# Memory keys and the middle chunks of residual projections: high and low inputs in one 512-column matmul

## The reference, cut to what matters

```python
# first block, twice: mixer A (selected attention), then mixer B (stick breaking)
x = layer_norm(ALPHA * x + (o * silu(g)) @ w_out, ln_g, ln_b)
# second block, two layers (fourier+neighbourhood mixer, then gated convolution)
m = rms_norm_2(mem, mem_norm_g)
h = h + mixer(rms_norm_2(h, mix_g)) @ w_out
k, v = split(m @ wkv)                    # memory keys and values
h = h + softmax(q @ k.T / 16) @ v @ wo   # q from rms_norm_2(h, xa_g) @ wq
h = h + conv_ffn(rms_norm_2(h, ffn_g))
return rms_norm_2(h, final_g)
```

## Time and profile before

| | us |
|---|---|
| median of three runs | 991.11 (990.96 to 991.43) |
| span of the profiled execution | 989.2 |
| PE busy | 972.1 (98%) |
| PE weight loads busy | 879.3 (89%) |
| DVE busy | 686.6 (69%) |
| ACT busy | 556.1 (56%) |
| POOL busy | 209.3 (21%) |

### The profile page before, as it was taken

How to read it: one execution, slowest core, us unless ns; L and a number is a source line. 1 busy time by engine, 2 the same in 40 slices (tenths; PEclk the granted TensorE clock), 3 DMA queues, 4 the chain that set the end, 5 groups by cost and what they waited for, 6 DMA issues and landing times.

```text
span 989.2 us, 16695 instructions
## 1 busy us (share of the span) xinstructions
PE 972.1 (98%) x6532; PEld 879.3 (89%) x6532; DVE 686.6 (69%) x1056; ACT 556.1 (56%) x856; POOL 209.3 (21%) x199
## 2 busy tenths in 40 slices
PE   9999989999999999999999999999999999999997
PEld 8779759989988988798899899999898989989985
DVE  5789785854666687665556779776687665767973
ACT  5556673665765474555355466555445555546662
POOL 0002034300344440012003005221044301202610
PEclk9999999999999999999999999999999999999999
DMA  9634425465334447246414655457546432555441
GB/s 363 241 132 166 175 87 208 162 221 214 128 128 141 174 133 271 108 171 213 150 64 170 213 186 187 181 194 281 186 170 255 163 135 93 198 183 181 172 152 43
DMA packets 24831, 172.93 MB, mean 175 GB/s; under 512 B 2752, under 2 KB 2880, under 8 KB 4416
## 3 DMA queue, kind: packets, MB, share of 16 engines
q1 hardware_dynamic: 23040, 160.66, 45.6%
q10 hardware_dynamic: 1728, 11.40, 3.0%
HBM read 166.81 MB, written 5.24 MB: 174 GB/s over the span
## 4 chain that ended last, share of the span: by engine, by line
PE 93%; DVE 2%; ACT 2%; DMA 1%; issue 1%; POOL 0%; SPq 0%; ACTq 0%; DVEq 0%
PE banks L506 38%; PE banks L594 16%; PE banks L512 14%; PE banks L514 7%; PE banks L504 6%; PE banks L656 4%; PE banks L710 1%; DMA raw<-w 1%; PE banks L761 1%; PE banks L762 1%; DVE work L1725 1%; PE banks L743 1%; PE banks L917 1%; PE banks L834 0%; DVE work L1737 0%
## 5 line engine op out<-in xcount | busy, mean ns | idle before, releaser
L1598 DVE TENSOR_TENSOR wl<-raw,wh 128x1024 fp32r<-128x1024 f32 x300 | 379.7, 1275 | 157.4 <-ACT wh L1090 156.0
L1090 ACT ACTIVATE wh<-raw 128x1024 fp32r<-128x1024 f32 x300 | 313.2, 1054 | 180.6 <-PE banks L506 76.1
L512 PE MATMUL banks<-xx,wh 128*128 128x512 f32 x544 | 192.5, 398 | 0.0
L506 PE MATMUL banks<-xx,wh 128*128 128x256 f32 x1024 | 190.3, 284 | 0.0
L506 PE MATMUL banks<-yy,wh 128*128 128x256 f32 x1024 | 187.8, 285 | 0.1
L506 PEld LDWEIGHTS banks<-xx,wh 128*128 128x128 f32 x1024 | 161.4, 192 | 1.4 <-issue 0.5
L506 PEld LDWEIGHTS banks<-yy,wh 128*128 128x128 f32 x1024 | 160.4, 192 | 0.7 <-issue 0.5
L514 PE MATMUL banks<-xx,wl 128*128 128x256 f32 x544 | 151.8, 279 | 0.0
L506 PE MATMUL banks<-xx,wl 128*128 128x256 f32 x512 | 144.8, 283 | 0.0
L506 PE MATMUL banks<-yy,wl 128*128 128x256 f32 x512 | 138.6, 283 | 0.0
L512 PEld LDWEIGHTS banks<-xx,wh 128*128 128x128 f32 x544 | 102.0, 187 | 22.7
(11 more groups left out here) (221 smaller groups left out, 1449.3 us busy)
## 6 DMA issues: line engine op xcount, KB each, us to landing
raw<-w SPq DMA_DIRECT2D x149, 1024.0 KB, 4.8
m_scratch<-yy ACTq DMA_DIRECT2D x2, 1024.0 KB, 5.9
k_scratch<-kt ACTq DMA_DIRECT2D x2, 1024.0 KB, 8.2
kt<-k_scratch ACTq DMA_DIRECT2D x2, 1024.0 KB, 5.8
yy<-m_scratch ACTq DMA_DIRECT2D x2, 1024.0 KB, 6.0
raw<-w SPq DMA_DIRECT2D x2, 512.0 KB, 5.2
h<-xt SPq DMA_DIRECT2D x2, 512.0 KB, 6.1
v<-memt ACTq DMA_DIRECT2D x1, 1024.0 KB, 7.7
```

The source lines that it names most:

```text
L506: return pe.matmul(b[:, j, :], weights, o_[:, kk, :], start=k0 + k == 0 and q == 0 and (j == 0 or not both_open), stop=k0 + k == KT * p.de ...
L512: pe.matmul(b[:, j, :], wh[:, slot, j, k * P:k * P + P], operand[:, :, tile0 + k0 + k, :], start=k0 + k == 0, stop=False, skip_group_check ...
L1090: act.activation(wh[:, n % 2, j, :], raw[:, n % RAW_SLOTS, j, :], ACT.Copy).then_inc(hi_ready, 1)
L1598: dve.tensor_tensor(wl[:, n % 2, j, :], raw[:, n % RAW_SLOTS, j, :], wh[:, n % 2, j, :].bitcast(F32), ALU.subtract).then_inc(lo_ready, 1)
```

## The change

The stages `kx0` and `kx1` become apart. With that, the pairs of `kx0`'s and `kx1`'s neighbours move, ACT gets a copy of the low part at the end of each key chunk's list, and DVE adds before it scales. In the residual projections `oa`, `ob`, `oab`, `oc`, `ox0`, `ox1` the chunks 1 and 2 (of 0 to 3) use 512-column matmuls into banks 6, 7 and 4, 5. DVE adds both parts to `h` straight from PSUM, in two instructions in place of one. Chunks 0 and 3 stay as they were. These stages are unrolled instead of looped, and chunk 2 is no longer in the early order.

```diff
-    add("kx0", 4, "dve")
+    add("kx0", 4, "dve", apart=True)
     add("gb", 4, "dve", apart=True)
...
-    add("kx1", 4, "dve")
+    add("kx1", 4, "dve", apart=True)
...
+        MIDDLE = {1: 6, 2: 4}
+
+        def middle_banks(c):
+            q = MIDDLE[c]
+            return banks[:, q:q + 2, 0:S], banks[:, q:q + 2, S:2 * S]
...
-            def project(name, operand, ready=None, hooks={}, tile0=0):
+            def project(name, operand, ready=None, hooks={}, tile0=0, middle=False):
...
+                        joined = middle and per * i + c in MIDDLE
+                        if joined:
+                            b = banks[:, MIDDLE[per * i + c]:, :]
...
-                                if apart and not early:
+                                if (apart or joined) and not early:
                                     mm = apart_product(k, j)
...
+                elif middle:
+                    round_(0, True)
+                    round_(1, False, {}, None)
...
-            project("oa", yy, y_ready("A", g_lo, GBASE["A"], 1))
+            project("oa", yy, y_ready("A", g_lo, GBASE["A"], 1), middle=True)
...
@@ ACT, layer_norm, at the end of each c
+                    act.wait_ge(w_used, 2 * n + 2)
+                    act.activation(kt[:, 2 * c:2 * c + 2, :], apart(p, c)[1], ACT.Copy).then_inc(low_out, 1)
...
@@ DVE, residual
                         elif alpha is None:
+                            if c in MIDDLE:
+                                b, low = middle_banks(c)
+                                chain(dve.tensor_tensor(hc, low, hc, ALU.add))
                             dve.tensor_tensor(hc, b, hc, ALU.add).then_inc(dve_evac, 1)
+                        elif c in MIDDLE:
+                            b, low = middle_banks(c)
+                            chain(dve.scalar_tensor_tensor(hc, hc, alpha, b, ALU.mult, ALU.add))
+                            dve.tensor_tensor(hc, low, hc, ALU.add).then_inc(dve_evac, 1)
...
@@ DVE, layer_norm, at the end of each c
-                    dve.wait_ge(w_used, 2 * n + 2)
-                    dve.tensor_tensor(kt[:, 2 * c:2 * c + 2, :], b3(p.pair + c % 2),
-                                      rb_m[:, :].unsqueeze(1).broadcast_to([P, 2, S]), ALU.mult).then_inc(dve_evac, 1)
+                    kc = kt[:, 2 * c:2 * c + 2, :]
+                    dve.wait_ge(low_out, LBASE[filler] + c + 1)
+                    chain(dve.tensor_tensor(kc, apart(p, c)[0], kc, ALU.add))
+                    dve.tensor_tensor(kc, kc, rb_m[:, :].unsqueeze(1).broadcast_to([P, 2, S]), ALU.mult).then_inc(dve_evac, 1)
```

More of the change, by code:

```diff
@@ L187 @@
 GEBASE = bases(("ffn0", 8), ("ffn1", 8))
-LBASE = bases(("gb", 4), ("qn", 2), ("kn", 2), ("qx0", 4), ("fu0", 8), ("cb", 4), ("cc", 4), ("qx1", 4), ("fu1", 8))
+LBASE = bases(("kx0", 4), ("gb", 4), ("kx1", 4), ("qn", 2), ("kn", 2), ("qx0", 4), ("fu0", 8), ("cb", 4), ("cc", 4), ("qx1", 4), ("fu1", 8))
 ACC = bases(*[(u, 4) for u in ("mem", "mean0", "var0", "mean1", "var1", "mix0", "xa0", "ffn0", "mix1", "xa1", "ffn1")])
@@ L993, in _ @@
                     z_values(t - 6)
-            project("ob", yy, y_ready("B", g_lo, GBASE["B"], 1))
+            project("ob", yy, y_ready("B", g_lo, GBASE["B"], 1), middle=True)
             project("kx1", yy, tile0=KT, hooks=layer_norm_hooks("1"))
@@ L1036, in _ @@
                            lambda a, b: [(bank[b][:, 0:S], slice(P * a, P * a + P))], 1, pn, "vn")
-            project("oab", yy, mixer_ready)
+            project("oab", yy, mixer_ready, middle=True)
             for l in "01":
@@ L1048, in _ @@
                 if l == "1":
-                    project("oc", yy, y_ready("conv", g_lo, GBASE["conv"], 2))
+                    project("oc", yy, y_ready("conv", g_lo, GBASE["conv"], 2), middle=True)
                 def first_scores(a, l=l):
@@ L1063, in _ @@
                                1, pa, "vx" + l)
-                project("ox" + l, yy, y_ready("X" + l, dve_evac, pa.base, 2))
+                project("ox" + l, yy, y_ready("X" + l, dve_evac, pa.base, 2), middle=True)
                 project("fu" + l, xx, x_ready("ffn" + l), hooks=norm_hooks("ffn" + l))
```

## The result

| | before | after |
|---|---|---|
| median (us) | 991.11 | 1006.21 (1005.45 to 1007.29, five executions) |
| ratio of the medians | | 1.0154 (1.0143 to 1.0165) |
| span of the profiled execution (us) | 989.2 | 1005.5 |
| its own time (us) | 991.1 (span plus 1.9) | 1007.29 |

The kernel became 1.5% slower, 15.1 us by the medians. The profiled execution is the longest of its five. All five have spans of 1003.6 to 1005.5 us, at mean granted clocks of 0.994 to 0.992, and the longer ones have the lower clock. The two profiles differ by 16.3 us.

What follows compares the result with a forecast made beforehand. PE, busy 98% of the span, was taken to bound the kernel. Terms 3.4 + 6.3 + 3.8 + 2.1 - 0.2 = 15.4 us on a 989.2 us span gave 1004.6, plus 1.9 for the median: 1006.5 us, range 1000.5 to 1009.5.

Steps and rivals of the forecast that it cites:

- `gb`: entry, with `oa` and `kx0`: At `gb`, PE waits for DVE's third key evacuation and starts near 197.1 us: +3.4 us, savings in `oa` and `kx0` included.
- clock behind it: Behind the waits at `gb` and `zf`, clock falls to 1.2 GHz for 3.9 us, losing 1.9 us each, +3.8 together.
- `zf`: entry, with `ob` and `kx1`: At `zf`, PE waits for `kx1`'s third evacuation until about 367.2 us; `zf` ends at 379.2, not 372.90: +6.3 us.
- the three statistics, with their savings: After `ox0`, `oc` and `ox1`, POOL's later sum delays PE's statistic, losing 0.7 us in each place, savings included: +2.1 us.
- I take 0.1 us later for DVE's list: In `kx0`, the shift expected of DVE's instruction list before its third key evacuation: 0.1 us.
- near 371: Sign to look for: PE idle before `zf`, 7 us long, near 371 us in the new trace's own time.
- The wait for the first chunk's banks: In `kx0`, PE waits 0.5 us at about 180.7 us for the first key chunk's evacuation before the third key chunk.
- The ring: In `ox0`, `oc`, `ox1`, DVE's and ACT's lists depend on each other in a cycle; third chunk's 0.7 us delay persists.
- The ring absorbs the third chunk's delay: Rival for `ox0`, `oc`, `ox1`: that delay is hidden too, 2.7 us less, 1003.8 us; 0.30 shared with a kinder clock.
- 0.9 us of waiting for POOL: Sign to look for: the statistic in `fu0`, `qx1` and `fu1` waits 0.9 us for POOL.
- DVE falls behind in `kx`: Rival in `kx0` and `kx1`: a late `lo` stops PE, two waits of 1.6 us, 1009.7 us; chance 0.10.
- The other side: Rival at `gb` and `zf`: DVE evacuates early enough, so entries and clock cost nothing, 991.0 or 988.3 us; chance 0.08.

Runs made afterwards that it cites:

- the half fill: Changed kernel plus 14 idle-work PE matmuls of 128 columns ahead of `gb`'s wait and 30 ahead of `zf`'s; 1003.58 us, ratio 1.0127.
- Own banks: Changed kernel, but `gb`'s first chunk and `zf` sum into free banks 6 and 7, so neither entry waits for the keys; 994.55 us, ratio 1.0034.
- the keys alone: Changed kernel with the residual projections as before, so only the memory keys in `kx0` and `kx1` are apart; 1006.69 us, ratio 1.0155.
- the middle chunks alone: Kernel before with only the second and third chunk of the six residual projections joined, keys as before; 991.95 us, ratio 1.0009.
- the earlier evacuation: Changed kernel with the third key chunk's copy and evacuation moved ahead of the last lo and last two low parts; 997.66 us, ratio 1.0067.

## Why the prediction was right

The forecast was 1006.5 us and the time is 1006.21. That the two agree within 0.3 us is luck: term by term the forecast is 0.9 us short of the profiled execution, and the median lies 1.1 us below that execution. The mechanism isn't luck, since every wait that it counted is there. By its own terms, with the places of the table above (in the time of the profile, which ended 1.1 us above the median of its kernel):

| term | forecast | shown |
|---|---|---|
| `gb`: entry, with `oa` and `kx0` | +3.4 | +3.9 |
| clock behind it | +1.9 | +1.5 |
| `zf`: entry, with `ob` and `kx1` | +6.3 | +6.9 |
| clock behind it | +1.9 | +2.7 |
| the three statistics, with their savings | +2.1 | +1.7 |
| `oab` | -0.2 | -0.2 |
| start of the trace | | -0.2 |
| sum | 15.4 | 16.3 |

These are one profiled execution's. The clock's share is the difference between the changed kernel's chunks and those of the half fill (7.51 less 6.01, 8.41 less 5.75); the entries are the rest of each pair of stages (5.20 + 0.59 - 0.34 = 5.45, and 9.36 + 0.36 - 0.19 = 9.53).

- **The mechanism at both entries** was as forecast: `gb`'s first matmul at 197.26 where about 197 stood, behind the third scaling, with idle times of 3.46 and 7.33 us released by DVE. Own banks took it away and the clock's loss with it; an earlier place in DVE's list shrank both.
- **"I take 0.1 us later for DVE's list"** was too little. It is 0.4 us in this trace's time and 0.6 with the 0.2 by which the trace started earlier. The statistic was forecast to be read at 184.7 to 185.1 and is at 185.13. This is most of what the two entries have too much. In the sum for `zf`, 10.9 us for its 48 matmuls doesn't follow from the two rows: with 3.00 for 12 and 5.55 for 24, the other 12 bring it to some 11.3, and the half fill's chain has 5.75 + 5.59 for them. And the sign "near 371" leaves out the clock behind `gb`: by the forecast's own terms it was to be about 372.5, and it is 372.88.
- **The wait for the first chunk's banks** in `kx` was forecast at 0.5 us. Between the two matmuls lie 0.90 us instead of 0.12, and the next one is another 0.1 late, so 0.9. It eats all that the joined tiles of `kx` save. By the distances of PE's matmuls two smaller things come on top: in `kx0` 22 of the 53 tiles that were forecast at 347 ns go at 353, behind this wait and behind the last spread (0.15 us), and the statistics take 0.2 to 0.3 us more of PE's time between joined tiles than between tiles of three. The entry hid all this in the changed kernel, and the versions without the entry wait pay it.
- **The clock**: forecast equal in both places, from the start of the trace. It isn't: 1.5 and 2.7 us here, and 0.8 and 0.2 more in the execution with the keys alone (8.35 and 8.62 us for the same matmuls, 5.3 us of work at the low clock at `gb`). At the longer standstill it had fallen well before PE began again and was low for 5.7 us of work, at the shorter one for 3.4. A single duration taken from the start of the program was the wrong measure; the sum was right within 0.5 because one term was too high and one too low, which is luck too.
- **The ring**: forecast 0.7 net in each of three places, shown 0.62, 0.48 and 0.62 in the changed kernel. That the second chunk's delay dies out and the third's arrives was shown by joining the second alone. *The ring absorbs the third chunk's delay* is refuted. The sign "0.9 us of waiting for POOL" came out as 0.47: of the 0.83 us by which `fu0` is longer, most of the rest is lost before, in one pause of 0.26 in its first chunk.
- **The pace** of the middle chunks: 353 ns, as forecast. By the Trainium skill, page TensorE: Matmul & The Clock Gate, section "Wait — 56ns, not 53.3ns?", a warm matmul of 512 columns is followed after about 216 ns, and by its formula one of 256 after 109: an estimate of 325 ns for the pair. The traces have 347 or 353 for the pair and 120 each for the 256-column ones, so the measured distances decide: the middle chunks alone saved 1.4 us, where by the section's figures it would be 0.5, an estimate from 12 x 16 tiles at 2.5 ns.
- **DVE falls behind in `kx`** didn't come true: no wait of PE for low weights in `kx0` or `kx1`. **The other side** neither, but it named the right lever. "It takes another order of DVE's list", and with it the time fell to 997.7. That even own banks leave it 0.3% slower than before was not in the forecast: the case was priced at 991.0, with the savings of `kx` in it that the wait above eats, and without the 1.4 us that `gb` and `zf` still lose to DVE's late queue.

Not settled: what of `zf`'s remaining 0.8 us with own banks is the low weights' lateness and what the pace, whether the longer executions of the earlier evacuation lost their time to the clock, and why the clock fell 2.4 us after the last matmul in one execution and 4.1 in another at the same place.

## What to carry to other kernels

A cheaper matmul form that needs its banks evacuated in two steps is priced at the reader: look up when the reader's list comes to that buffer today, not how long the step takes. Here the steps cost 0.7 us, and their place in DVE's list 3.5 and 7.3. A standstill of PE can also cost the work behind it: 1.5 and 2.7 us here, 2.3 us with the keys alone at the place of the 1.5, and nothing behind 0.9 us. And spend the form by slack: the same two-step evacuation is free where the next statistic has room, and costs 0.7 to 0.8 us where it is already tied to another engine.

## What the runs showed of the hardware

- Pairs of a 512- and a 256-column fp32r matmul keep one of two mean paces, 353 or 347 ns, for whole chunks. A float32 matmul of one column put between moved 48 tiles from the slower to the faster one (16.61 us for them where 16.96 stood); an fp32r matmul of 256 columns did not (16.86).
- A float32 matmul of 128 columns is recorded as two, 0.11 us apart: 28 records in 3.29 us for the 14 matmuls of the half fill.
- In the changed kernel the granted clock fell 3.0 us after the start of the last matmul at `zf`, but 4.1 us after it at `gb`, when PE was already at work again. With the keys alone, at the same place in `gb` and with a standstill only 0.1 us longer, it fell after 2.4 us. Where the standstill was 2.54 us it stayed at 1.00 in the profiled execution. Back at work, it was low for 3.4 us at `gb` and 5.7 us at `zf`, and for 5.3 us at `gb` with the keys alone.
